# Two mixers of a two-layer decoder step: prompt heads in pairs, group norm by a centring product, gates and squares moved

## The reference

```
# layer 0, mixer: RWKV-7 (8 heads x 64) and a gated MLP, then one output projection
y   = scan(s_t = s w + (s.-kk) kka + v k ; y_t = s.r)           # per head
mu  = mean(y); var = mean((y - mu)^2)                           # over the 64 of a head
ya  = ((y - mu) * rsqrt(var + eps) * lnx_g + lnx_b + bonus) * g # g: a low-rank gate
x   = x + concat(ya, yb) @ w_out
# layer 1, mixer: gated recurrence (RG-LRU) and dilated attention (8 heads x 64)
xc  = conv4(x_b);  r, i = sigmoid(xc @ rgate), sigmoid(xc @ igate)   # 8 blocks each
a   = exp(-8 r softplus(-lambda));  b = sqrt(1 - a^2) * i * xc
h_t = a h_(t-1) + b_t ;  yc = gelu(gy) * h
p   = softmax(q k^T / 8 + bias);  o = p v                       # prompt: 256 x 256 per head
x   = x + concat(yc, o) @ w_out
```

## Time and profile before

| | |
|---|---|
| median of 3 runs | 1008.15 us (1006.0 to 1008.88) |
| the profiled execution, its own time | 1006.7 us |
| its span, first to last instruction | 1004.8 us |
| TensorE clock granted, mean share of full | 0.997 |
| PE, PEld, DVE, ACT, POOL busy | 984.4, 839.2, 804.3, 642.2, 25.5 us |

### The profile page before, as it was taken

The page is one execution under the profiler, slowest core; times in us unless marked ns, Lnnn a source line. Parts: engine busy times, 40 slices in busy tenths (PEclk is TensorE's granted clock), DMA queues, the critical chain, the costliest instruction groups (busy, mean ns, idle before and its releaser), DMA issues.

```text
span 1004.8 us, 17469 instructions
## 1 busy us (share of the span) xinstructions
PE 984.4 (98%) x7316; PEld 839.2 (84%) x7316; DVE 804.3 (80%) x925; ACT 642.2 (64%) x695; POOL 25.5 (3%) x30
## 2 busy tenths in 40 slices
PE   9999999999999999999999999999999999999996
PEld 8899999787888888888879877798888888888884
DVE  7777643768989989989985676776998998998994
ACT  6685234657777777777664443654877777777673
POOL 0000100000000000000004000000000000000000
PEclk9999999999999999999999999999999999999998
DMA  9533000282999999999949679626499999999951
GB/s 369 190 124 128 3 4 6 88 334 72 382 364 356 367 361 366 355 375 367 369 145 411 263 292 386 236 87 250 173 372 372 368 367 364 365 366 363 366 227 54
DMA packets 40465, 271.48 MB, mean 270 GB/s; under 512 B 5072, under 2 KB 5408, under 8 KB 9664
## 3 DMA queue, kind: packets, MB, share of 16 engines
q1 hardware_dynamic: 39760, 267.56, 69.9%
q0 software_dynamic: 624, 2.76, 0.7%
HBM read 266.23 MB, written 4.07 MB: 269 GB/s over the span
## 4 chain that ended last, share of the span: by engine, by line
PE 85%; DVE 7%; ACT 4%; DMA 1%; issue 1%; ACTq 0%; POOL 0%; DVEq 0%; POOLq 0%
PE ps L996 11%; PE ps L998 11%; PE ps L997 11%; PE ps L1030 6%; PE ps L1031 6%; PE ps L1032 6%; PE ps L357 3%; PE ps L1965 3%; PE ps L359 3%; PE ps L358 3%; DMA raw<-in_stream 1%; PE ps L1009 1%; PE ps L3117 1%; DVE w_lo L351 1%; ACT w_hi L341 1%
## 5 line engine op out<-in xcount | busy, mean ns | idle before, releaser
L351 DVE TENSOR_TENSOR w_lo<-raw,w_hi 128x2048 fp32r<-128x2048 f32 x74 | 171.3, 2315 | 30.1 <-ACT w_hi L341 30.1
L341 ACT ACTIVATE w_hi<-raw 128x2048 fp32r<-128x2048 f32 x72 | 137.6, 1914 | 57.4 <-PE ps L998 21.3
L351 DVE TENSOR_TENSOR lo_more<-raw_more,hi_more 128x2048 fp32r<-128x2048 f32 x48 | 109.8, 2288 | 14.0 <-ACT hi_more L341 14.0
L351 DVE TENSOR_TENSOR w_lo<-raw_more,w_hi 128x2048 fp32r<-128x2048 f32 x47 | 107.5, 2290 | 14.0 <-ACT w_hi L341 14.0
L351 DVE TENSOR_TENSOR lo_more<-raw,hi_more 128x2048 fp32r<-128x2048 f32 x48 | 109.9, 2290 | 10.7 <-ACT hi_more L341 10.7
L341 ACT ACTIVATE hi_more<-raw 128x2048 fp32r<-128x2048 f32 x48 | 91.9, 1915 | 23.9 <-PE ps L998 23.9
L341 ACT ACTIVATE w_hi<-raw_more 128x2048 fp32r<-128x2048 f32 x47 | 90.1, 1917 | 15.6 <-PE ps L1032 15.6
L341 ACT ACTIVATE hi_more<-raw_more 128x2048 fp32r<-128x2048 f32 x48 | 91.9, 1915 | 9.6 <-PE ps L1032 9.6
L357 PE MATMUL ps<-h_hi,w_hi 128*128 128x320 f32 x272 | 86.4, 318 | 0.7 <-DVE arena L2746 0.7
L359 PE MATMUL ps<-h_hi,w_lo 128*128 128x320 f32 x272 | 84.0, 309 | 0.0
L358 PE MATMUL ps<-h_lo,w_hi 128*128 128x320 f32 x272 | 84.0, 309 | 0.0
(11 more groups left out here) (564 smaller groups left out, 2335.9 us busy)
## 6 DMA issues: line engine op xcount, KB each, us to landing
raw<-in_stream SPq DMA_DIRECT2D x125, 1024.0 KB, 6.9
raw_more<-in_stream SPq DMA_DIRECT2D x96, 1024.0 KB, 6.9
arena<-in_k_near SPq DMA_DIRECT2D x6, 1024.0 KB, 9.9
arena<-in_v_near SPq DMA_DIRECT2D x5, 1024.0 KB, 6.9
arena<-in_k_far SPq DMA_DIRECT2D x6, 512.0 KB, 8.3
kv_spare<-in_v_near SPq DMA_DIRECT2D x3, 1024.0 KB, 8.7
arena<-in_v_far SPq DMA_DIRECT2D x5, 512.0 KB, 6.0
kv_spare<-in_k_near SPq DMA_DIRECT2D x2, 1024.0 KB, 13.1
```

Of the source, the lines that this page charges most:

```text
L341: eng.activation(hi_slot(W_SLOT[c]), raw_chunk(c), ACT.Copy).then_inc(S("w_hi_made"), 1)
L351: eng.tensor_tensor(lo_slot(W_SLOT[c]), raw_chunk(c), hi_slot(W_SLOT[c]), ALU.subtract).then_inc(S("w_lo_made"), 1)
```

## The change

It has four parts. **Pairs.** `prompt_scores`, `prompt_turn` and `prompt_values` take the two heads of a slice together: scores of head 2j in bank 2 from partitions 0 to 63, of head 2j + 1 in bank 3 from partitions 64 to 127, matmul by matmul in turns; transposes go back into the same two banks; values in turns to output partitions 0 to 63 and 64 to 127. **Gates.** They are called earlier, two by two, between tiles 15 and 18 (after tiles 15, 16 and 17), and `UNITS` with them. **Centring.** `head_ones` becomes ident - head_ones / 64, so that the product gives y - mu; ScalarE squares it out of PSUM in two halves, VectorE scales it by lnx_g out of PSUM; lnx_b is added to the bonus by ScalarE inside the state update; the low part of the two output chunks is made in halves, partly inside blocks 2 and 3; `own_solved` goes from ScalarE to GpSimd; a small Sqrt brings the table load ahead. GpSimd takes `own_solved` between `unit_matrices` and the DMA of out_wkv_p; TensorE takes the first `out0_rows` of the new order ahead of its wait for `y_made`. **Squares.** `lru_square` is an activation on ScalarE, again with a small Sqrt ahead of the root.

```diff
-            "s_out1", "p_scores6", "p_turned5", "p_out4", "s_scores3",
+            "s_out1", "p_out4", "p_out5", "p_scores6", "p_scores7", "gate1", "gate5", "s_scores3",
...
+            for n in range(2):
+                eng.wait_ge(S("head_sums"), 2 * n + 2)
+                eng.activation(s5[:, 2 * n:2 * n + 2, :], ps[:, 2 * n:2 * n + 2, 0:T], ACT.Square).then_inc(S("gn_sq"), 1)
+            own_values(eng, range(1))
             eng.wait_ge(S("mix0_sums"), 3)
-            eng.activation(gn_root, ps[:, 0, 0:Q], ACT.Sqrt, bias=eps_gn, scale=1.0 / 64).then_inc(S("gn_root"), 1)
-            own_solved(eng, range(NB))
+            eng.activation(gn_root, ps[:, OUT0_BANK[3], 0:Q], ACT.Sqrt, bias=eps_gn, scale=1.0 / 64).then_inc(S("gn_root"), 1)
+            own_values(eng, range(1, NB))
...
+            eng.scalar_tensor_tensor(head_ones, head_ones, -1.0 / 64, ident, ALU.mult, ALU.add).then_inc(S("mix0_vector"), 1)
...
-            eng.scalar_tensor_tensor(s1, ps[:, 0:4, 0:T], -1.0 / 64, s1, ALU.mult, ALU.add).then_inc(S("mix0_vector"), 1)
-            eng.wait_ge(S("mix0_vector"), MIX0_VECTOR["gn_centred"])
-            eng.tensor_tensor(s5, s1, s1, ALU.mult).then_inc(S("gn_sq"), 1)
-            split_lo(eng, AT_OUT0 + 1)
+            out_low(eng, AT_OUT0 + 1, 0)
+            for j in range(HT):
+                eng.wait_ge(S("gn_sq"), j // 2 + 1)
+                last = eng.tensor_scalar(s1[:, j, :], ps[:, j, 0:T], par("lnx_g", j), None, ALU.mult)
...
+            out_low(eng, AT_OUT0 + 1, 1).then_inc(S("w_lo_made"), 1)
             eng.wait_ge(S("mix0_spread"), 3)
-            for j in range(HT):
-                v = quartered(s1[:, j, :])
-                last = eng.scalar_tensor_tensor(v, v, par("lnx_g", j), spread_of(0, j), ALU.mult, ALU.mult)
+            for n in range(2):
+                v = s1[:, two(n), :].rearrange("p j (t q) -> p j t q", t=4)
+                last = eng.tensor_tensor(v, v, ps[:, 0:4, 2 * Q * n:2 * Q * n + 2 * Q].rearrange("p t (j q) -> p j t q", j=2), ALU.mult)
...
-            for j in range(HT):
-                last = eng.scalar_tensor_tensor(s1[:, j, :], s1[:, j, :], par("lnx_b", j), R_T[:, j, :], ALU.add, ALU.add)
+            for n in range(2):
+                last = eng.tensor_tensor(s1[:, two(n), :], s1[:, two(n), :], R_T[:, two(n), :], ALU.add)
...
-            out0_rows(eng, 0, (4, 5, 6, 7), True, False)
-            out0_rows(eng, 1, (4, 5), True, False)
...
+            out0_rows(eng, 0, (4,), True, False)
...
+            out0_rows(eng, 0, (5, 6, 7), False, False)
+            eng.wait_ge(S("gn_sq"), 2)
+            head_sums(eng, OUT0_BANK[3], s5).then_inc(S("mix0_sums"), 1)
+            out0_rows(eng, 1, (4, 5, 6), True, False)
...
+            eng.wait_ge(S("mix0_vector"), MIX0_VECTOR["bonus_made"])
+            for j in range(HT):
+                eng.activation(R_T[:, j, :], R_T[:, j, :], ACT.Identity, bias=par("lnx_b", j))
...
+            eng.activation(small[:, 327:328], eps_gn, ACT.Sqrt)
             y_kept(3)
...
-        def own_solved(eng, bs):
+        def own_solved(eng):
 
             sum_ready(eng, 2, "q_low")
+            eng.wait_ge(S("y_made"), 4)
+            for b in range(NB):
+                mine = const("own_batch", TS)[:, b:b + 1].unsqueeze(2).unsqueeze(3).broadcast_to((TS, 2, HT, 64))
+                eng.tensor_tensor(qv[0:TS, :, b, :].rearrange("p (j w) v -> p w j v", w=2), q_all[0:TS].rearrange("p (w j) v -> p w j v", w=2), mine,
+                                  ALU.mult).then_inc(S("qe_made"), 1)
...
-        UNITS = [("tile", t) for t in range(18)] + [("gate", j) for j in range(HT)] + [("tile", 18)]\
-            + [("gate", HT + j) for j in range(HT)] + [("tile", 19)]
+        UNITS = [("tile", t) for t in range(16)] + [("gate", 0), ("gate", 4), ("tile", 16), ("gate", 1), ("gate", 5), ("tile", 17)]\
+            + [("gate", j) for j in (2, 6, 3, 7)] + [("tile", 18), ("tile", 19)]
...
+        PAIR = ((0, 2), (64, 3))
...
+            eng.activation(lru_t, lru_a, ACT.Square).then_inc(S("mix1_scalar"), 1)
             out_half(0).then_inc(S("mix1_scalar"), 1)
...
+            eng.activation(small[:, 327:328], eps_norm, ACT.Sqrt)
+            vector_did(eng, "lru_sum")
             eng.activation(lru_m, lru_m, ACT.Sqrt, scale=0.25).then_inc(S("mix1_scalar"), 1)
...
+            def prompt_scores(j):
+                if j:
+                    scalar_did(eng, f"p_tok{2 * j - 1}")
+                for o, bank in PAIR:
+                    eng.matmul(ps[:, bank, 0:P], q1[o:o + 64, j, 0:P], k1[o:o + 64, j, 0:P], start=True, stop=True)
+                for o, bank in PAIR:
+                    eng.matmul(ps[:, bank, P:384], q1[o:o + 64, j, P:TP], k1[o:o + 64, j, 0:TP], start=True, stop=True).then_inc(S("mix1_tensor"), 1)
```

More of the change, by code:

```diff
@@ L1870, in mix0_pe @@
             wkv_pe(eng)
+            eng.wait_ge(S("y_lo"), 1)
+            out0_rows(eng, 0, (4,), True, False)
             eng.wait_ge(S("y_made"), 4)
@@ L3074, in v1_turn @@
                     mm.then_inc(S("mix1_tensor"), 1)
-            def prompt_scores(h):
-                o, j = 64 * (h % 2), h // 2
-                if h:
-                    vector_did(eng, f"p_max{h - 1}")
-                eng.matmul(ps[:, SCORE_BANK, 0:P], q1[o:o + 64, j, 0:P], k1[o:o + 64, j, 0:P], start=True, stop=True)
-                eng.matmul(ps[:, SCORE_BANK, P:384], q1[o:o + 64, j, P:TP], k1[o:o + 64, j, 0:TP], start=True, stop=True).then_inc(S("mix1_tensor"), 1)
-            def prompt_turn(h):
-                vector_did(eng, f"p_normed{h}")
-                if h:
-                    scalar_did(eng, f"p_tok{h - 1}")
-                for i in range(3):
-                    mm = eng.transpose(ps[:, TURN_P_BANK, P * i:P * i + P], score_p[:, h % 2, P * i:P * i + P], ident)
-                mm.then_inc(S("mix1_tensor"), 1)
@@ new lines, in prompt_turn, with prompt_values @@
+            def prompt_turn(j):
+                for r, (o, bank) in enumerate(PAIR):
+                    vector_did(eng, f"p_normed{2 * j + r}")
+                    for i in range(3):
+                        mm = eng.transpose(ps[:, bank, P * i:P * i + P], score_p[:, r, P * i:P * i + P], ident)
+                    mm.then_inc(S("mix1_tensor"), 1)
+            def prompt_values(j):
+                if j:
+                    vector_did(eng, f"p_kept{j - 1}")
+                else:
+                    scalar_did(eng, "v1_tok2")
+                scalar_did(eng, f"p_tok{2 * j + 1}")
+                for to, rows, at, start, stop in ((slice(0, P), 0, 0, True, True), (slice(P, TP), 0, P, True, False), (slice(P, TP), 1, TP, False, True)):
+                    for r, (o, _) in enumerate(PAIR):
+                        mm = eng.matmul(ps[o:o + 64, OUT_P_BANK, to], v1_tok[:, rows, P * j + o:P * j + o + 64], pt_p[r][:, at:at + P], start=start, stop=stop)
+                        if stop and not start:
+                            mm.then_inc(S("mix1_tensor"), 1)
@@ L3204, in mix1_pe @@
             sample_turn(1)
-            prompt_scores(5)
-            prompt_turn(4)
-            prompt_values(3)
+            prompt_turn(2)
+            gate(0)
+            gate(4)
             sample_values(1)
@@ L3211, in mix1_pe @@
             sample_out(1)
-            prompt_scores(6)
-            prompt_turn(5)
-            prompt_values(4)
+            prompt_values(2)
+            prompt_scores(3)
+            gate(1)
+            gate(5)
             sample_scores(3)
@@ L3399, in _ @@
             unit_matrices(eng)
+            own_solved(eng)
             eng.wait_ge(S("state_made"), 5)
```

187 lines of the change are left out of this document (78 added, 109 removed), and 23 rows, old and new, of tables (MIX1_SCALAR, MIX1_TENSOR, MIX1_VECTOR).

## The result

| | before | after |
|---|---|---|
| median, us | 1007.97 (4 runs, 1006.0 to 1008.88) | 999.25 (4 runs, 998.76 to 1000.96) |
| profiled execution, us | 1006.7 | 999.15 |
| its span, us | 1004.8 | 997.3 |
| TensorE busy, us | 984.4 | 978.1 |

The ratio is 0.9919, 95% interval 0.99 to 0.9938: 8.2 us less, with 6.2 to 10.1 as its bounds (the two medians lie 8.7 apart). The forecast was 999.0, 8.6 us of gain worked out. In a later set of runs of the same kernel the ratio was 0.9915 (0.9902 to 0.9928). So the sum came out; some of its parts did not, and the two profiled executions show it only when they are laid side by side.

The account below looks back on a forecast made before the run. TensorE, busy 984.4 of 1004.8 us, was taken to bound the kernel. Gains of 6.1 + 2.5 = 8.6 us took the profiled 1006.7 to 998.1, the median 1008.15 to 999.5; 999.0 was chosen, range 995.5 to 1003.5.

Parts of the forecast that it names:

- Pairs: Second mixer: two heads' scores or values together cost about what one head did, taking 6.6 us off TensorE's list.
- The transposes: Second mixer: the second head's transposes follow without a switch, saving 0.4 us (an estimate, 0 to 0.6).
- TensorE up to tile 19: Second mixer: 8.7 us gained less 0.85 of new stalls, so tile 19 starts 7.9 us earlier, at 645.8.
- Both old waits: Second mixer: TensorE's idle places of 0.80 and 0.90 us, both claimed to go.
- the walk: Second mixer: new instruction lists stepped through with old durations; new stalls of 0.35 and 0.5 us at `sample_values(3)` and `sample_out(3)`.
- The chain behind it: End of second mixer: ScalarE's serial work holds the output projection until 650.9, leaving a gain of 6.1 us (4.5 to 7.9).
- Key and value buffers: Second mixer: loads arrive in time, slack below 1 us; put at 0, with 0.5 to 2 us at stake.
- End of the first mixer: First mixer up to `sample_adds`: it ends at 190.5 instead of 193.01, a gain of 2.5 us (0.5 to 3.6).
- 1.0 on the path: First mixer: VectorE's two-SBUF-input instructions wait for GpSimd, costing 1.0 us; 2.5 if it strikes twice.
- The rival that GpSimd holds the samples' update: First mixer: slow `own_solved` instructions delay `sample_adds`; at 3 us each the kernel takes 1013; chance 0.05.
- 8 (x - 1.27): First mixer: wait of `sample_adds` if a GpSimd instruction takes x us; eats the whole 8.6 us gain at x = 2.35.
- The experts' stages ... shift as they are.: Experts' stages: they run at TensorE's own pace and only move in time, with no gain or loss.

Follow-up runs that it names:

- both_mended: Changed kernel with output-row products among the router's small ones in both layers, spare k/v buffer second, attention copies earlier; 995.63 us, ratio 0.9879 to before.
- after_again: The changed kernel unaltered, run again for more executions; 999.37 us.
- square_vector: The changed kernel with the square of the decay back on VectorE instead of ScalarE; 998.95 us.
- own_scalar: The changed kernel with own_solved moved from GpSimd back to ScalarE, behind own_values; 1003.72 us.

## Why the prediction was right

- **Pairs.** Shown: 0.86 and 0.80 us a pair, as the rows of one head said. 6.6 was forecast, 3.52 + 3.10 = 6.6 measured. The transposes were a mis-sized term: 0.4 forecast, 1.04 measured (six in a row take 0.63 us where two heads apart took 0.96; why is not shown).
- **TensorE up to tile 19.** Both old waits went. The new ones came where the walk put them: `sample_values(3)` 0.36 (0.35 forecast), `sample_out(3)` 0.23 (0.5). Tile 19 starts at 644.02, which with the lead of 1.6 us on entry is 645.6 on before's clock; 645.8 was forecast. That this fits so well is partly luck: the 0.64 us that the transposes gave beyond the forecast were eaten by 0.6 of longer sample values, `sample_out` and gates, which the walk did not have.
- **The chain behind it.** Shown in place and size: TensorE stands 1.77 us, forecast about 1.5; 6.1 us for the mixer were forecast, 6.0 measured, and `both_mended`, which moves work out of ScalarE's and VectorE's end, gives the 1.8 us back. Within it I took the square and the early Sqrt for worth more than they are, in the experiments' expectations rather than in the sum.
- **Key and value buffers.** Put at 0; a wait of 0.17 us in after, 0.38 in `after_again`, 0 in `square_vector`. The slack is as thin as the row said: an execution may lose a few tenths, and the profiled one of `both_mended` lost 1.37.
- **End of the first mixer.** 2.5 forecast, 3.0 measured. Sums done at 179.3 (179.0), spread 181.9 (181.5), scaled 183.5 (183.7), `ya_made` 188.1 (187.9). Wrong was the term "1.0 on the path" for GpSimd. The collision is real and cost VectorE 0.84 us, but on the path it cost nothing: VectorE waited for TensorE's gate product behind it either way, 0.61 us in after and 1.45 in `own_scalar`. `ya_made` at 188.1 is the time forecast for an undisturbed VectorE, and that is why 3.0 came instead of 2.5. Wrong too was the last step: `qe_made` did not come at 188.4 to 188.9 but with GpSimd's last instruction at 184.49, and `sample_adds` began at 188.13 right behind TensorE's own rows and VectorE's last multiply (188.07). In the text I had let eight instructions of 1.27 end at 185 and then set a later time for them without a reason. The rival that GpSimd holds the samples' update was far off: 1.19 us an instruction. Its price, 8 (x - 1.27), also left out the 3 us between 185 and 188, so that x would have had to be higher than 2.35.
- **"The experts' stages ... shift as they are."** This step failed in the pair of profiled executions: 1.5 us were lost in the first router. It holds once executions without a clock drop are compared: 9.2 us in all, 0.6 above the forecast (0.5 of the first mixer, 0.2 that `after_again` was ahead at 168 us already, and 0.1 less from the second mixer). The median hid it: the profiled execution of before was one without a drop, 1.45 us below its median, and I added 0.9 of that at the end without a cause. So 999.0 beside a measured 999.25 is closer than the working deserved, and that is luck: the 0.6 that the gain was too small and the 0.9 added at the end make up the 1.5 us of a drop that the forecast did not know of.

## What to carry to other kernels

Add up the time from start to start of each kind of product in both traces, and set the n-th instruction of one beside the n-th of the other: it shows within a tenth of a us where a lead is won and lost, which no view of waits does when the clock is the cause. Before a difference of 1 or 2 us between two profiles is explained, read the granted clock in small windows in both, and look at how single executions group. When TensorE gets ahead of a serial end of ScalarE and VectorE, look at what of that end could have been done in their earlier waits: here three quarters of a copy and a subtraction moved into idle places, and the last copy put ahead of the gelu, gave back 1.8 us. Where another engine makes an instruction longer, look at what the step behind it waits for before its price goes on the path: here 0.84 us vanished in a wait.

## What the runs showed of the hardware that I had not expected

- Products of two row tiles pass one another: with the list in the order A, A', B, B', the records of A and B start 0.014 us apart and the pair takes 0.87 us, as in turns. Products of two column tiles in head order take 1.07 instead of 0.80.
- TensorE's clock falls to 1.2 GHz for some 3 us, 0.1 to 1.2 us behind the end of the router's small products, in some executions of a kernel and not in others: at 217, 220, 222, 681 or 685 us, or nowhere; and once at 191 us, 0.3 us after a standstill of 2.5 us. Each time in a router costs about 1.5 us.
- ScalarE's table load of 1.28 us does not wait for what the activation behind it waits for, and the activation follows it within 0.01 us (643.12 behind 641.83 + 1.28). An early small activation helped only where it stood in an earlier idle place of ScalarE (172.79 in place of 179.17, 0.5 us), and not where it stood right ahead of that wait.
- Two additions of 640 columns with both inputs in SBUF take 1.56 us alone and 2.40 when they begin 0.98 us before the end of GpSimd's instructions.
